# First attention: VectorE scales step 0 of each pair of heads before it takes the minima of step 1

## The reference

```python
s_win = jnp.einsum('bcqhd,bicjhd->bhcqij', q_r, k_r).astype(jnp.float32) + bias
s_win = s_win.reshape(B, N_HEADS, ncb, NA_QCB, n_win)
s_ctx = jnp.einsum('bcqhd,bkhd->bhcqk', q_r, kc).astype(jnp.float32)
p = jax.nn.softmax(jnp.concatenate([s_win, s_ctx], axis=-1), axis=-1).astype(v.dtype)
...
o = (jnp.einsum('bhcqij,bicjhd->bcqhd', p_win, v_r)
     + jnp.einsum('bhcqk,bkhd->bcqhd', p_ctx, vc))
...
s = jnp.einsum('bqhgd,bkhd->bhgqk', qg, kc).astype(jnp.float32)
p = jax.nn.softmax(s, axis=-1)[..., :C].astype(vc.dtype)
o = jnp.einsum('bhgqk,bkhd->bqhgd', p, vc)
```

## Time and profile before

| | us |
|---|---|
| median of 3 runs | 2650.8 (2648.41 to 2651.13) |
| the profiled execution | 2650.28 |
| its span, first to last instruction | 2648.6 |
| TensorE's matmuls busy in the span | 2600.7 |
| VectorE busy | 1663.6 |
| ScalarE busy | 1093.3 |
| first attention with its edges | 528 to 627 |

### The profile page before, as it was taken

One profiled execution on the slowest core, in us unless ns is written; L12 is line 12 of the kernel. 1 busy time (PEld: TensorE's weight loads), 2 busy tenths in 40 slices (PEclk: granted clock), 3 DMA queues, 4 the chain that ended last, 5 costly groups with the idle time before them and its releaser, 6 DMA issues.

```text
span 2648.6 us, 43300 instructions
## 1 busy us (share of the span) xinstructions
PE 2600.7 (98%) x17036; PEld 2307.5 (87%) x17036; DVE 1663.6 (63%) x2506; ACT 1093.3 (41%) x1559; POOL 434.2 (16%) x483
## 2 busy tenths in 40 slices
PE   8999999999999999999999989999999999999999
PEld 6888888967888889888889789989999999998999
DVE  6766746465774474675666765567666666665565
ACT  3222224275421223321224664454555545555453
POOL 4000034123400004200015030021001201100210
PEclk9999999999999999999999999999999999999999
DMA  7554524411353351453442135545424554532554
GB/s 293 175 177 160 193 90 152 151 57 57 111 194 117 111 192 70 158 199 129 157 171 95 39 112 199 187 168 188 148 96 150 185 199 163 183 135 80 179 187 152
DMA packets 64761, 394.40 MB, mean 149 GB/s; under 512 B 7552, under 2 KB 9056, under 8 KB 29664
## 3 DMA queue, kind: packets, MB, share of 16 engines
q1 hardware_dynamic: 43872, 317.17, 33.8%
q0 software_dynamic: 20192, 73.21, 8.4%
q10 hardware_dynamic: 544, 1.89, 0.2%
HBM read 391.19 MB, written 1.05 MB: 148 GB/s over the span
## 4 chain that ended last, share of the span: by engine, by line
PE 86%; DVE 6%; ACT 3%; issue 2%; POOL 1%; DMA 1%; SPq 1%; DVEq 0%; ACTq 0%; POOLq 0%
PE banks L454 23%; PE banks L456 23%; PE banks L455 23%; DVE wlo L379 2%; PE banks L571 1%; PE banks L573 1%; PE banks L572 1%; ACT whi L371 1%; PE banks L1633 1%; PE banks L1644 1%; PE banks L1657 1%; PE banks L474 1%; PE banks L476 1%; PE banks L475 1%; DVE h L979 1%
## 5 line engine op out<-in xcount | busy, mean ns | idle before, releaser
L379 DVE TENSOR_TENSOR wlo<-raw,whi 128x2048 fp32r<-128x2048 f32 (+1 forms) x262 | 639.9, 2442 | 349.8 <-ACT whi L371 349.7
L371 ACT CAST whi<-raw 128x2048 fp32r<-128x2048 f32 (+1 forms) x262 | 530.1, 2023 | 447.6 <-PE banks L456 407.0
L454 PE MATMUL banks<-uhi,whi 128*128 128x512 f32 (+1 forms) x1520 | 551.4, 363 | 3.1 <-DVE wlo L379 1.5
L455 PE MATMUL banks<-ulo,whi 128*128 128x512 f32 (+1 forms) x1520 | 550.3, 362 | 0.0
L456 PE MATMUL banks<-uhi,wlo 128*128 128x512 f32 (+1 forms) x1520 | 550.2, 362 | 0.0
L454 PE MATMUL banks<-u2hi,whi 128*128 128x256 f32 x1248 | 355.8, 285 | 0.6 <-DVE wlo L379 0.5
L455 PE MATMUL banks<-u2lo,whi 128*128 128x256 f32 x1248 | 352.3, 282 | 0.0
L456 PE MATMUL banks<-u2hi,wlo 128*128 128x256 f32 x1248 | 352.3, 282 | 0.0
L616 DVE SCALAR_TENSOR_TENSOR squares<-mod_slot,crow 128x1024 f32<-128x1024 f32 x256 | 313.3, 1224 | 32.4 <-DMA mod_slot<-in_w_mod 9.1
L454 PEld LDWEIGHTS banks<-uhi,whi 128*128 128x128 f32 x1520 | 285.1, 188 | 54.1 <-issue 1.8
L456 PEld LDWEIGHTS banks<-uhi,wlo 128*128 128x128 f32 x1520 | 285.1, 188 | 50.1
(11 more groups left out here) (458 smaller groups left out, 4885.6 us busy)
## 6 DMA issues: line engine op xcount, KB each, us to landing
raw<-in_ffn_in SPq DMA_DIRECT2D x132, 1024.0 KB, 4.9
raw<-in_ffn_out SPq DMA_DIRECT2D x48, 1408.0 KB, 6.4
mod_slot<-in_w_mod POOLq DMA_DIRECT2D x128, 512.0 KB, 3.7
raw<-in_w_merge SPq DMA_DIRECT2D x32, 1024.0 KB, 4.8
raw<-in_w_in SPq DMA_DIRECT2D x26, 1024.0 KB, 4.8
raw<-in_na_qkv SPq DMA_DIRECT2D x12, 1024.0 KB, 4.8
raw<-in_w_out SPq DMA_DIRECT2D x8, 1024.0 KB, 4.8
raw<-in_wa_qkv SPq DMA_DIRECT2D x6, 1024.0 KB, 4.7
```

Source lines behind the costliest of these rows:

```text
L371: act.copy(whi[u % 2][:, 0:unit_size[u]], raw[u % 2][:, 0:unit_size[u]]).then_inc(hi_done, 1)
L379: dve.tensor_tensor(wlo[u % 2][:, 0:n], raw[u % 2][:, 0:n], whi[u % 2][:, 0:n].bitcast(F32), ALU.subtract).then_inc(lo_done, 1)
L454: pe.matmul(out, w_hi, x_hi[:, k, 0:T], start=(n == 0), stop=False)
L455: pe.matmul(out, w_hi, x_lo[:, k, 0:T], start=False, stop=False)
```

## The change

In `attention_dve`, for the first attention only and only when n is step 1 of a pair (`n % 4 == 1`), the minima of step n are written behind the scaling of step n-1 (step 0 of the pair) instead of ahead of it. Nothing is added or taken away, and the waits are the same ones.

```diff
@@ -1727,7 +1727,8 @@
     def attention_dve(dve, tag, steps, y_hi, y_lo):
         N = len(steps)
         for n in range(N + 3):
-            if n < N:
+            norm_first = tag == "L0" and n % 4 == 1
+            if n < N and not norm_first:
                 dve.wait_ge(*PE_.at(tag, "scores", n))
                 attention_max_dve(dve, tag, steps, n)
             if 1 <= n <= N:
@@ -1745,6 +1746,9 @@
                     pr = probs(m, side)[:, 0:t["n"]]
                     dve.tensor_scalar(pr, pr, inv[:, side:side + 1], None, ALU.mult)\
                         .then_inc(*DVE_.up((tag, "probs", m, side)))
+            if n < N and norm_first:
+                dve.wait_ge(*PE_.at(tag, "scores", n))
+                attention_max_dve(dve, tag, steps, n)
             if n >= 3 and steps[n - 3]["last"]:
                 t = steps[n - 3]
                 dve.wait_ge(*ACT_.at(tag, "out", t["group"]))
```

## The result

| | before | changed |
|---|---|---|
| median, us | 2647.49 (2641.68 to 2652.37, 20 runs) | 2653.14 (2646.97 to 2656.97, 20 runs) |
| profiled execution, span | 2650.28, 2648.6 | 2655.37, 2653.7 |
| one turn of the first attention, pair 1 | 10.51 | 10.84 |
| one turn, pairs 2 to 6, each | 10.51 | 11.28 |
| last pair, from its first scores to the projection | 13.93 | 14.56 |

The ratio is 1.0020, with a 95% interval of 1.0014 to 1.0027: the change costs about 5.3 us (3.7 to 7.1). The forecast of 2653.4 us lies beside the measured 2653.14, but that is luck: over 20 runs the kernel before came out at 2647.5, 3.3 us under the median of three runs from which the sum was made. By what the change does, the forecast was +2.6 and the result is about twice that. The lengths in the table are differences of start times of TensorE's blocks.

The account below looks back on a forecast made before the run. TensorE's stream was taken as the bound (busy 2600.7 of 2648.6 us); 6 x 0.32 = 1.9 for pairs 1 to 6 plus 0.65 for pair 7 gave +2.6, forecast 2653.4 us (+0.1%), range 2649.5 to 2656.0.

Parts of the forecast that it names:

- The stall removed: TensorE's transposes of step 0, waiting for VectorE's scaled rows, start 0.70 us earlier; taken alone 7 x 0.70 = 4.9 us.
- Minima of step 1 later by 1.11: On VectorE, step 1's minima start when step 0's two scalings are through, at 606.87 instead of 605.76.
- keeps its slack: GpSimd's bias for step 1 is wanted 3.7 us later; the move shifts its releases by at most about 1 us.
- Scores of step 3 wait: On TensorE, step 3's scores wait for ScalarE's exponentials of step 1, start 609.69; 0.67 of the 0.70 is given back.
- Transposes of step 1 later, behind the copies, by 0.32: On TensorE, they wait for ScalarE's copies of step 0, 610.68 against 610.36; turn 10.84, pairs 1 to 6 together 1.9 us.
- Last pair +0.65: In pair 7 no scores follow to cover ScalarE's 0.68 delay, so step 2's transposes start at 623.56 instead of 622.91.
- rival (c): Delay runs round the turn through ScalarE's copies of step 1; full 1.11 a turn, 7.8 us, 2658.6; chance 0.06.
- Rival (a): The stall before step 0's transposes goes and nothing comes in its place; -4.9 us, 2645.9; chance 0.05.
- (b): Break-even: the scores wait, but ScalarE's copies do not come last; 2650.6 us; chance 0.12.
- Rival (d): TensorE's clock falls to half rate for one stretch of 10.3 us, costing 5.1 more; 2658.5 us; chance 0.04.
- The bounds of the unknown costs: -0.2 us if the copies did not come last; +4.8 if ScalarE's whole 0.68 came through in every turn.
- the 0.10 for more than 0.2%: Chance that the whole kernel measures slower than 2656.1 us, beyond the 0.2% (5.3 us) a measurement can tell from no change.

## Why the prediction was right and wrong

**The stall removed: right.** The 7 waits before the transposes of step 0 are gone, and no other takes their place there.

**Minima of step 1 later by 1.11: wrong, and this is the step that failed.** The term was "606.08 + 0.79 (607.51 to 608.30)". The 0.79 is true of the place it was read at, where GpSimd stood still. At the new place the scalings run beside GpSimd's tile and take 1.28 (599.56 - 598.28); with the tile out of the way they take 0.80 (597.58 - 596.78). The minima start 1.60 later in the turn than before (5.47 after its start against 3.87), and 1.13 later with the tile out of the way (597.58 - 592.58 = 5.00). That 0.48 comes through to the turn nearly whole, because from here on the chain minima, exponentials, scores of step 3 has no slack: the exponentials of step 1 wait for VectorE, and TensorE for the exponentials. 5 pairs x 0.46 (11.28 - 10.82) = 2.3 of the 2.4 us.

**GpSimd "keeps its slack": the right question was not asked.** The bias did come in time, as forecast. But the paragraph on GpSimd looked only at when its result is wanted, not at what its instruction would run beside. The place could have been worked out from before: its tile runs there beside the reduction, 3.88 us into the turn (605.77 - 601.89), and the first scaling 5.62 into it (607.51 - 601.89).

```profile
605.77 0.72 POOL L1954 TENSOR_TENSOR mod_slot<-k,mod_slot 128x256 f32<-128x256 f32 x1 [1.98 <-DMA mod_slot<-in_na_rpb]
```

The forecast itself moved that scaling to 606.08, 4.19 into the turn and 0.31 behind the start of a 0.72 tile. The Trainium skill (SBUF — State Buffer, section "Who interferes with whom") has the rule that prices it: a VectorE scaling in its two-port mode and a GpSimd instruction share a port pair, whoever issues first holds it for a whole instruction, and the other is blocked. The trace agrees: one scaling goes from 0.48 to 0.95, or GpSimd's 0.72 to 0.91, depending on who was first, and this tile beside a reduction out of the banks keeps its 0.72. It does not agree that all the time beside the other is lost: in pair 1 the tile's last 0.23 cost 0.04. By the Trainium skill's rule alone the scaling at 606.08 would have stood until the tile's end at 606.49, an estimate of 0.41 a turn, 6 x 0.41 = 2.5 us on top of the 2.6. I did not weigh it.

That 2.5 lies near the measured 2.4, but not for its own reason. A scaling that came second ended 0.28 after the tile in these runs (last section), so a tile at its old place would have cost 606.49 + 0.28 - 606.56 = 0.21 a turn, an estimate of 1.3 us in all. The scaling came where it was forecast, 4.19 into the turn (598.28 - 594.09), but the tile moved as well: it starts 4.29 into the turn (598.38 - 594.09; 4.14 to 4.32 in pairs 2 to 6) instead of 3.88. Its load is started behind the bias tile before it, and that tile waits for a scaling of VectorE which now ends later in the turn: it starts 0.51 into the turn, and started 0.15 into it before (602.04 - 601.89). "The move shifts its releases by at most about 1 us" was true, and 0.4 of it was enough to put the tile where it cost 0.46 a turn.

```profile
594.60 0.72 POOL L1958 TENSOR_TENSOR mod_slot<-k,mod_slot 128x256 f32<-128x256 f32 x1 [1.65 <-DVE scaled L1747]
```

**Scores of step 3 wait: right in kind, and without the overlap in size.** "0.67 of the 0.70 is given back here", as a wait of some 0.6: it is 0.58 with GpSimd's tile out of the way, and 1.05 with it.

**Transposes of step 1 later, behind the copies, by 0.32: right.** The wait is 0.26 in the list, the turn without the overlap 10.81 to 10.82 against 10.84, and the halved copies take the wait away. The one turn of the changed kernel in which GpSimd's tile cost a scaling only 0.04 measured 10.84.

**Last pair +0.65: right**, 14.56 - 13.93 = 0.63, with and without the overlap, since in pair 7 both scalings kept their 0.49 and 0.48. The sum of the steps, +2.6, measured +2.4 where the overlap is taken out.

**The rest.** VectorE idles 0.43 before the reciprocal of step 0 (forecast about 0.4). The first block behind the attention starts at 631.21, and at 626.34 in before: 4.9 later where 2.6 was forecast. By the test in the prediction a turn above 11.2 would have proved rival (c), the delay that runs round the turn. The turn of 11.28 did not: (c) needed 0.80 more on ScalarE's copies of step 1, and the list of waits has no wait behind these copies (`mod_slot`) but the last pair's; what came was a longer scaling on VectorE. The test was too loose; a length alone names no mechanism. Rival (a), nothing in the stall's place, is out, and so is (b). Rival (d), a falling clock, is out for the attention: the granted clock is 1.00 in the turn that stands still most, 1.31 us in two pieces.

**Chances and range.** The range of 2649.5 to 2656.0 holds 2653.14, helped by the lower level of the 20 runs. The bounds of the unknown costs, -0.2 to +4.8 us, only just reach the +4.8 measured in the attention and not the +5.3 of the whole kernel, and the upper one was argued from ScalarE, not from the cause that came. The ratio, 1.0014 to 1.0027, lies across the 0.2% that the prediction called no change. With the chain alone this was unlikely, as forecast; the 0.10 for more than 0.2% left the overlap out.

## What to carry to other kernels

A duration read from a trace belongs to its neighbours as well as to its instruction: when an instruction moves, look up what every engine runs at the new place, GpSimd above all, and if a VectorE operation from SBUF to SBUF now falls on a GpSimd instruction, expect whichever comes second to last until some time after the other's end (0.28 us for the scaling, 0.58 for the tile here). The neighbour's place is to be worked out too, since the change can move it: here it went 0.4 us later in the turn. When a wait of the critical engine is removed by putting one chain ahead of another on a shared in-order engine, follow the chain that was put behind, and everything queued behind it on the next engine, before booking the gain. Where both chains are wanted at once, split them: filling the pieces into each other's gaps gained 1.5 to 1.7 us of the attention here (too little to show in the whole kernel's time), where swapping them whole lost 4.8.

## What the runs showed of the hardware

- A blocked instruction does not show as idle time or a wait. It shows as a longer instruction: 0.48 to 0.95 for a 512-wide scaling, 0.72 to 0.91 or 1.01 for a GpSimd tile. The list of waits has no line for it; a group's mean (653 ns for 484) and the busy time of a stretch with the same count do.
- Who came first decided, to within hundredths. GpSimd tiles that started up to 0.04 after the scaling by the records still came first (564.08 beside 564.07, 596.97 beside 596.93); at 0.05 (564.50 beside 564.45), 0.09 (586.14 beside 586.05) and 0.16 (575.31 beside 575.15) they came second. So the same code has turns of 10.54 and of 11.08 in one execution.
- The one that came second ended a fixed time after the other, in every overlap of these runs that held one up. A scaling ended 0.28 to 0.29 after the tile: 598.28 + 1.35 - (598.38 + 0.97) = 0.28, 565.09 - 564.80 = 0.29, 587.00 - 586.72 = 0.28. A full tile ended 0.58 to 0.59 after the scaling: 576.22 - 575.64 = 0.58, 608.86 - 608.27 = 0.59. A scaling is 0.48 alone and a tile 0.72, so some 0.2 and 0.14 of each was done before or beside the other.
- Beside the reduction, which reads from the banks, GpSimd's tile kept its 0.72, with starts 0.01 apart.
- An independent reciprocal between the reduction and the fused addition that depends on it took no time (0.72 from start to start with it, 0.71 to 0.73 without).
- One execution had its 128x512 matmuls at four times their length from the start on at a granted clock of 1.00, and from 4152 us on at 1.00 to 1.16 us each at one of 0.26, while VectorE's scalings kept their 0.48. Its cause stays open; a second run of the same kernel did not have it.
